# First expert layer of a two-layer mixture of experts: token rows picked by TensorE in blocks of 32 instead of scattered to memory and read back in blocks of 64

## The chip, the cores and the metric

The kernel runs on one core of a Trainium2 chip. The metric is the device time of one execution in microseconds. TensorE does the matrix products and transposes, VectorE (DVE), ScalarE (ACT) and GpSimd (POOL) the elementwise work, and SyncE (SP) issues most of the DMAs. All numbers are fp32.

## The reference

A first model of two layers (feed forward, mixer, feed forward, gated embedding) is followed by a second one whose two layers each have attention and a mixture of 32 experts. The change is in the experts of the second model's layer 0, where 512 tokens (256 of the sequence, 256 of the context) are routed:

```python
lg = t @ wr_g + br_g;  g = argmax(lg)                  # one of 4 groups
le_g = (t @ wr_e + br_e) of that group                 # 8 experts of it
top_v, top_i = top_k(le_g, 2)                          # two experts a token
weights = softmax(lg)[g] * softmax(top_v)
hidden = silu(x @ w_gate[e]) * (x @ w_up[e])           # x: rows of expert e, 1024 wide; hidden 512 wide
out[token] += weight * (hidden @ w_down[e])
```

Here `t` is `rmsnorm(x) * g * (1 + scale) + shift`, with shift and scale of its own for the sequence and for the context. The reference's own routing of its inputs gives the 32 experts of layer 0 these numbers of rows: 39 32 34 30 33 35 34 43, 35 39 27 38 41 37 29 38, 32 31 29 27 37 22 22 34, 32 33 31 30 26 24 29 21, 1,024 in all. In layer 1 (256 tokens) no expert has more than 26.

## The kernel before

Each engine has a program of its own, and semaphores order them. The three weights of an expert (gate, up, down, 2 MB each) are loaded by SP into nine slots, three experts deep: `sp_experts` issues the loads of expert e+3 when `moe_ended` of expert e is up. In layer 1 ten slots are used (`sp_experts_rows`).

Layer 0 before the change. The output projection `pe_project_out` (L1754) makes eight column tiles, VectorE adds them to x (L1767), and the sums of squares follow each (L1370). Then `act_modulated` and `dve_modulated` make the normed tokens (L1404, L1409, L1391), `pe_router` makes the logits (L1960) and turns all tokens to rows (L1971, copied out at L1994), and `dve_router` chooses experts and places (`dve_choice`, L2009 to L2078). GpSimd scatters every token's row twice into the buffer `expert_in` in memory (`pool_scatter`, L2104). Both buffers in memory are zeroed long before, in the first model's mixers (L875).

The expert loop runs one block of 64 rows a turn; the number of blocks of an expert is known only on the chip, so each expert has a loop whose two bounds are loaded to registers of each engine (`first_block`, L2110). With the counts above every expert has one block. Each turn: gate and up products (L2155; two groups of 64 columns at a time), the next block's rows turned (L2121, copied out at L2129), silu on ScalarE (L2185), the product with up on VectorE (L2203), its transpose (L2162, copied out at L2208), the down products (L2169), and the result copied by ScalarE (L2189) and written by its DMA queue to `expert_out` in two DMAs (L2192). ScalarE also loads the rows of the block after the next (L2136). L2172 ends an expert. After the last one GpSimd gathers two rows a token (L2218, L2221), and they are weighed, turned and added (L2229, L2238, L2244).

Layer 1 already works with blocks of 32 rows. Its loop has gate and up (L2468, four groups of 32 columns at a time), a pick of the next block's rows (L2429) copied out by ScalarE (L2515) and turned (L2436), a transpose (L2486) copied out at L2580, the down products (L2492), and two `pe_put` steps (L2444) with their own transposes (L2480), which layer 0 does not get. Silu is L2513, the product with up L2576.

Of the kernel before, what the change touches and what calls it, by code (L numbers as in the profile page):

```python
# [24 lines left out]
BLOCK = (64, 32)  # L25
LAM_INIT = 0.8 - 0.6

MAXROWS = max(bl * NE + 2 * n for bl, n in zip(BLOCK, (2 * S, S)))
# [5 lines left out]
class Signal:  # L34
# [29 lines left out]
    "pe_router": "r_logits r_turned r_rows_turned r_counted r_summed", "pe_moe": "moe_ended moe_turned", "pe_rows": "xr_turned xr_prepared acc_done",  # L64
# [4 lines left out]
    "act_moe": "moe_weighed", "act_rows": "xr_squared xr_out xr_root", "act_final": "final_squared final_root",  # L69
# [5 lines left out]
    "dve_moe": "moe_combined moe_added", "dve_rows": "xr_step", "dve_final": "final_step",  # L75

    "pool_setup": "zeros_set upad_zero", "pool_squares": "squares conv_u", "pool_moe": "pool_ended",
# [5 lines left out]
slot0 slot1 slot2 slot3 slot4 slot5 slot6 slot7 slot8 slot9 const3 gain_in sink_in router_in gathered0 gathered1 gathered2 gathered3 scattered stored  # L83
""".split()

BLOCKS = "x_in x_turned x_ready gated silu hidden h_turned h_ready down y_ready y_out".split()
# [29 lines left out]
def second_constants():  # L116
# [15 lines left out]
    def window(q0):  # L132
# [5 lines left out]
        "multiples": np.tile(np.arange(1, 8), (P, 1)), "swa0": window(0), "swa1": window(P),  # L138
# [20 lines left out]
class Kernel:  # L159
# [35 lines left out]
    def first_memory(self):  # L195
# [43 lines left out]
        self.xbuf = self.nc.dram_tensor("expert_in", [MAXROWS + 2 * P, D], F32).ap()  # L239
# [20 lines left out]
    def second_memory(self):  # L260
# [22 lines left out]
        self.router_cols = (KT + 1) * 36  # L283
# [554 lines left out]
def sp_mixer(k, l):  # L838
# [32 lines left out]
    for buf in (k.xbuf, k.ybuf):  # L871
        n = buf.shape[0] // P // DEPTH
        rows = buf.rearrange("(n p) d -> p n d", p=P)
        for d in (0, D // 2):
            sp.dma_start(rows[:, l * n:(l + 1) * n, d:d + D // 2], k.zeros.unsqueeze(1).broadcast_to([P, n, D // 2])).then_inc(*s["zeroed"].up(l, d, buf is k.xbuf))  # L875
# [868 lines left out]
def pe_project_out(k, l, first, slots, src, ntok):  # L1744
    pe, s = k.nc.tensor, k.s
    for j in range(KT):
        slot = slots[j // 4]
        w = chunk_view(k, slot, 512)
        if j % 4 == 0:
            pe.wait_ge(*s[f"slot{slot}"].at("chunk", first + j // 4))  # L1750
        if j >= 4:
            pe.wait_ge(*s["out_added"].at(l, j - 4))
        for t in range(KT):
            last = pe.matmul(k.ps[:, j % 4, 0:ntok], w[:, t, (j % 4) * P:(j % 4 + 1) * P], src[:, t, 0:ntok], start=(t == 0), stop=(t == KT - 1), skip_group_check=True)  # L1754
        last.then_inc(*s["out_tile"].up(l, j))
        if j > 0:
            pe_sums(k, f"moe{l}", j - 1, ntok)
    pe_sums(k, f"moe{l}", KT - 1, ntok)


def dve_project_out(k, l, streams):
    V, s = k.nc.vector, k.s
    for j in range(KT):
        V.wait_ge(*s["out_tile"].at(l, j))
        for st in streams:
            X = k.x[:, j, st * S:(st + 1) * S]
            last = V.scalar_tensor_tensor(X, k.ps[:, j % 4, st * S:(st + 1) * S], k.mod_col(l, 2, j, st), X, ALU.mult, ALU.add)  # L1767
        last.then_inc(*s["out_added"].up(l, j))


def act_project_out(k, l, ntok):
    act, s = k.nc.scalar, k.s
    for j in range(KT):
        act.wait_ge(*s["out_added"].at(l, j))
        act_square(k, f"moe{l}", j, ntok)


# [3 lines left out]
class Routing:  # L1781


    def __init__(self, k, l):
        self.numbers(l)
        self.V, self.at, self.end = k.Vflat, k.router_cols, 4096 - 2304
        self.wr, self.bias = self.V[:, 0:KT * 36].rearrange("p (k e) -> p k e", k=KT), self.V[:, KT * 36:k.router_cols]
        self.count_banks = (0, 5, 6)
        self.choice_tiles()
        nt = self.nt  # L1790
        self.idest, self.started = self.small(2, nt).bitcast(I32), self.small(len(BLOCKS))
        kf = self.V[:, 4096 - 2304:]
        BL, F, W = self.BL, self.F, self.W
        self.logits = kf[:, 0:self.T]
        self.xe = kf[:, 0:W]
        self.xeT = kf[:, 512:512 + KT * BL].rearrange("p (k s) -> p k s", k=KT)
        self.sil = kf[:, 1024:1024 + F]
        self.hb = kf[:, 1280:1280 + F]
        self.hT = kf[:, 1536:1536 + 4 * BL].rearrange("p (f s) -> p f s", f=4)
        self.yb = kf[:, 1792:1792 + W]  # L1800
        self.rows = k.Qflat[:, 0:nt * D].rearrange("p (t d) -> p t d", t=nt)
        self.g2 = k.Kflat.rearrange("p (t d) -> p t d", t=4)
        self.n = {n: Signal(k, f"moe{l}_{n}", [k.stack.enter_context(k.nc.semaphore(f"moe{l}_{n}")), 0]) for n in BLOCKS}

# [6 lines left out]
    def choice_tiles(self):  # L1811
# [7 lines left out]
        self.over = self.small(8)  # L1819
        self.pos, self.dest = self.small(nt, 32), self.small(2, nt)  # L1820
        self.ge = self.small(nt, 4)

    def small(self, *shape):
        n = int(np.prod(shape))
        v = self.V[:, self.at:self.at + n]
# [64 lines left out]
def expert_slots(e):  # L1890
    return ((2, 3, 4), (5, 0, 1), (6, 7, 8))[e % 3]
# [962 lines left out]
```

## Time and profile before

| | us |
|---|---|
| three runs, median (range) | 3088.99 (3086.84 to 3089.89) |
| the profiled execution's own time | 3092.75 |
| its span, first to last instruction | 3091.4 |
| first gate product of layer 0's experts starts | 1819.85 |
| last down product of layer 0's experts ends | 2352.9 |
| granted clock, mean of the span | 0.952 |

Times in the rows below are microseconds from the start of the span. The difference of 1.35 between the own time and the span lies outside the instructions. A shift of everything behind layer 0's experts moves the time by as much.

### The profile page before, as it was taken

To read this page: it belongs to the slowest core of one execution; us is meant where nothing else is said; L and a number is where in the kernel's file an instruction comes from. 1 tells how busy PE (TensorE), PEld (TensorE's weight loads), DVE (VectorE), ACT (ScalarE), POOL (GpSimd) and SP (SyncE) were. 2 spreads that over 40 slices of the span, in tenths; PEclk is the share of its full clock that TensorE was granted. 3 is DMA by queue.
4 is the path that set the end of the run, shared out by engine and by line. 5 is a ranking of instruction groups with operands and counts; after the bars stand their busy time and mean duration, and the time that the engine had idled before them with its cause. 6 is when DMAs were issued, how large, how long until landed. Compare 5 with 4: busy or idle time off the path is not lost.

```text
span 3091.4 us, 43046 instructions
## 1 busy us (share of the span) xinstructions
PE 2688.8 (87%) x17970; PEld 1901.5 (62%) x17970; DVE 723.0 (23%) x1844; ACT 462.0 (15%) x1096; POOL 103.8 (3%) x146
## 2 busy tenths in 40 slices
PE   8999999999999999997997868777775998877676
PEld 7888788887888688883445434343433566544454
DVE  2003420022003420023128221000002253332223
ACT  2001310011002310012016120000001142000001
POOL 1001010011001010010000010000001000000000
PEclk9999999999999999998999979989997998999989
DMA  7544765556544765525120169999997214999997
GB/s 266 189 144 146 265 219 181 168 172 204 179 135 164 262 218 195 186 86 202 55 82 1 55 234 398 397 402 398 398 397 262 92 55 171 371 420 419 420 419 310
DMA packets 257036, 721.47 MB, mean 233 GB/s; under 512 B 14207, under 2 KB 141902, under 8 KB 232270
## 3 DMA queue, kind: packets, MB, share of 16 engines
q1 hardware_dynamic: 237760, 691.74, 59.7%
q10 hardware_dynamic: 16782, 18.60, 1.9%
q0 software_dynamic: 2304, 8.39, 0.7%
q8 instruction: 145, 2.38, 0.3%
q14 instruction: 45, 0.37, 0.0%
HBM read 678.84 MB, written 39.85 MB: 232 GB/s over the span
## 4 chain that ended last, share of the span: by engine, by line
PE 71%; DMA 16%; DVE 6%; ACT 3%; issue 3%; ACTq 0%; POOL 0%; SPq 0%; DVEq 0%; POOLq 0%
PE ps L663 18%; DMA arena<-in_moe_w_up 15%; PE ps L674 10%; PE ps L1444 6%; PE ps L2155 5%; PE ps L2468 3%; PE ps L1490 2%; PE ps L2169 2%; PE ps L895 2%; PE ps L687 2%; PE ps L1055 2%; PE ps L1754 2%; PE ps L2429 1%; PE ps L2492 1%; PE ps L2274 1%
## 5 line engine op out<-in xcount | busy, mean ns | idle before, releaser
L663 PE MATMUL ps<-arena 128*128 128x256 f32 x2560 | 568.6, 379 | 3.5 <-DVE arena L745 3.5
L663 PEld LDWEIGHTS ps<-arena 128*128 128x128 f32 x2560 | 482.9, 189 | 73.9 <-issue 4.1
L2155 PE MATMUL ps<-arena 128*64 128x256 f32 x2048 | 259.3, 416 | 78.9 <-issue 77.9
L674 PE MATMUL ps<-arena 128*128 128x256 f32 x1408 | 317.9, 379 | 0.0
L674 PEld LDWEIGHTS ps<-arena 128*128 128x128 f32 x1408 | 264.8, 189 | 46.2 <-issue 8.4
L2155 PEld LDWEIGHTS ps<-arena 128*64 128x64 f32 x2048 | 159.8, 150 | 166.5 <-issue 107.3
L2468 PE MATMUL ps<-arena 128*32 128x128 f32 x4096 | 143.3, 299 | 75.8 <-issue 74.2
L1444 PE MATMUL ps<-arena 128*128 128x512 f32 (+2 forms) x512 | 192.8, 548 | 11.3 <-ACT arena L1391 11.2
L787 DVE TENSOR_TENSOR arena<-arena,ps 128x256 f32<-128x256 f32 x76 | 32.0, 422 | 638.4 <-ACT arena L755 633.8
L2468 PEld LDWEIGHTS ps<-arena 128*32 128x32 f32 x4096 | 128.6, 121 | 85.2 <-issue 83.3
L1444 PEld LDWEIGHTS ps<-arena 128*128 128x128 f32 (+1 forms) x512 | 89.4, 179 | 104.9 <-issue 97.5
L2169 PE MATMUL ps<-arena 128*64 128x512 f32 x512 | 117.0, 596 | 18.1 <-issue 18.1
L2203 DVE TENSOR_TENSOR arena<-arena,ps 128x256 f32<-128x256 f32 x32 | 19.2, 599 | 479.6 <-ACT arena L2185 479.6
L755 ACT ACTIVATE arena<-ps 128x256 f32<-128x256 f32 x76 | 29.2, 384 | 675.1 <-PE ps L663 675.1
L2492 PE MATMUL ps<-arena 128*32 128x256 f32 x1024 | 62.1, 381 | 35.9 <-DVE arena L2580 35.9
L2169 PEld LDWEIGHTS ps<-arena 128*64 128x64 f32 x512 | 40.2, 136 | 74.2 <-issue 74.2
L532 POOL TENSOR_TENSOR arena<-arena 128x256 f32<-128x256 f32 x64 | 42.8, 671 | 1079.9 <-DVE arena L500 1070.6
L895 PE MATMUL ps<-arena 128*128 128x256 f32 x352 | 77.4, 379 | 0.0
L2429 PE MATMUL ps<-arena 128*32 128x256 f32 x528 | 70.4, 637 | 7.6 <-issue 4.3
L895 PEld LDWEIGHTS ps<-arena 128*128 128x128 f32 x352 | 66.3, 189 | 9.5
L2492 PEld LDWEIGHTS ps<-arena 128*32 128x32 f32 x1024 | 36.1, 109 | 53.9 <-issue 42.3
L1490 PE MATMUL ps<-arena 128*128 128x512 f32 (+1 forms) x192 | 69.2, 520 | 0.0
(411 smaller groups left out, 2811.6 us busy)
## 6 DMA issues: line engine op xcount, KB each, us to landing
arena<-in_moe_w_gate SPq DMA_DIRECT2D x64, 2048.0 KB, 31.3
arena<-in_moe_w_up SPq DMA_DIRECT2D x64, 2048.0 KB, 31.1
arena<-in_moe_w_down SPq DMA_DIRECT2D x64, 2048.0 KB, 34.9
arena<-in_mod_w SPq DMA_DIRECT2D x24, 2048.0 KB, 13.4
arena<-in_w_gate SPq DMA_DIRECT2D x44, 1024.0 KB, 5.5
arena<-in_w_up SPq DMA_DIRECT2D x44, 1024.0 KB, 8.1
arena<-in_w_down SPq DMA_DIRECT2D x44, 1024.0 KB, 4.9
expert_in<-arena SPq DMA_DIRECT2D x4, 3328.0 KB, 14.6
```

What stands on the lines that cost most here:

```text
L663: last = pe.matmul(k.ps[:, T % 4, off:off + S], w[:, t, T % 2 * P:(T % 2 + 1) * P], h[:, t, :], start=(t == 0), stop=(t == KT - 1), skip_g ...
L674: last = pe.matmul(acc[:, t, :], d[:, T % 2, t * P:(t + 1) * P], k.hid[:, T % 4, :], start=(T == 0 and t % 2 == 0), stop=end, skip_group_c ...
L687: last = pe.matmul(k.ps[:, T, off:off + S], w[:, t, T * P:(T + 1) * P], k.hu[:, t, :], start=(t == 0 and off == 0), stop=(t == KT - 1), sk ...
L895: last = pe.matmul(dst, w[:, t, j * P:(j + 1) * P], src[:, t, :], start=(t == 0), stop=(t == KT - 1), skip_group_check=True)
L1055: last = pe.matmul(k.banks(4, 4, S)[:, j, :], w[:, t, (j % 2) * P:(j % 2 + 1) * P], k.y[:, t, :], start=(t == 0), stop=(t == KT - 1), skip ...
L1444: last = pe.matmul(k.ps[o:o + m, j % 4, 0:ntok], w[:, t, c0:c0 + m], k.h2[:, t, 0:ntok], start=(t == 0), stop=(t == KT - 1), tile_position ...
L1490: last = pe.matmul(k.ps[:, 6 + n % 2, 0:m], k.h2[:, i, t * P:(t + 1) * P], w[:, i, :], start=(i == 0), stop=(i == KT - 1), skip_group_chec ...
L2155: last = pe.matmul(ps[BL * q:BL * q + BL, b, 0:F], m.xeT[:, t, :], wv[:, t, F * q:F * q + F], start=(t == 0), stop=(t == KT - 1), tile_pos ...
L2169: last = pe.matmul(ps[BL * q:BL * q + BL, 3, 0:W], m.hT[:, f, :], wd[:, f, W * q:W * q + W], start=(f == 0), stop=(f == 3), tile_position= ...
L2429: last = k.nc.tensor.matmul(k.ps[32 * q:32 * q + 32, bank, 0:256], m.pick[:, t, :], rows, start=(t == 0), stop=(t == 1), tile_position=(0, ...
L2468: last = pe.matmul(ps[BL * q:BL * q + BL, 0, a:a + F], m.xeT[:, t, :], wv[:, t, F * q:F * q + F], start=(t == 0), stop=(t == KT - 1), tile ...
L2492: last = pe.matmul(ps[BL * q:BL * q + BL, 3, 0:W], m.hT[:, f, :], wd[:, f, W * q:W * q + W], start=(f == 0), stop=(f == 3), tile_position= ...
```

## The change

The tokens are no longer normed and modulated as columns. While the output projection runs, TensorE also makes the logits from x itself with weights multiplied by the gains, sums of squares by one-column products, and transposes of x times its gain; the shift is made into rows once. ScalarE copies the turned halves out (the second with the factor 1/rms), GpSimd adds the shift, and the token rows stay on chip (`rows`, in the space of h). The scatter, the buffer `expert_in`, its zeroing and its loads go away.

Blocks have 32 rows. VectorE makes a 0/1 matrix of places (`dve_places`), TensorE multiplies it with the rows (`pe_pick_rows`), ScalarE copies the block, TensorE turns it (`pe_turn_picked`), VectorE copies it out. The pick and the turning of the next block stand behind the down products of this one. The result is written in four DMAs of 32 KB instead of two of 128 KB. Expert 2's down weights take slot 9 instead of 8, and its three loads wait for the rows' making, the last column's turning and the projection's end. The loads of layer 1's projection weights wait for experts 30 and 31 instead of for the gathers. The zeroed part of `expert_out` becomes smaller.

```diff
-BLOCK = (64, 32)
+BLOCK = (32, 32)
-        self.xbuf = self.nc.dram_tensor("expert_in", [MAXROWS + 2 * P, D], F32).ap()
 def expert_slots(e):
-    return ((2, 3, 4), (5, 0, 1), (6, 7, 8))[e % 3]
+    return ((2, 3, 4), (5, 0, 1), (6, 7, 9))[e % 3]
...
+def pe_token_sums(k, m, i):
+    pe.wait_ge(*s["out_added"].at(0, i))
+    for t in range(4):
+        pe.matmul(k.ps[:, 3, 36 * t:36 * t + 36], k.x[:, i, t * P:(t + 1) * P], m.wp[:, t // 2, i, :], start=False, stop=(i == KT - 1), skip_group_check=True)
+    pe.wait_ge(*s["xs_squared"].at(i))
+    for t in range(4):
+        last = pe.matmul(k.ps[:, 3, 144 + t:145 + t], k.sqb[:, i % 4, t * P:(t + 1) * P], k.c["ones"][:, 0:1], start=False, stop=(i == KT - 1), skip_group_check=True)
...
+def pool_rows(k, m):
+    for t in range(4):
+        pool.wait_ge(*s["xs_out"].at(t, 1))
+        row = permuted(m.rows[:, t, :], 1)
+        pool.tensor_tensor(row, row, permuted(m.shift_rows[:, t // 2, :], 1), ALU.add).then_inc(*s["rows_made"].up(t, 1))
+    for t in range(4):
+        pool.wait_ge(*s["xs_row"].at(t))
+        row = permuted(m.rows[:, t, :], 0)
+        pool.tensor_tensor(row, row, permuted(m.shift_rows[:, t // 2, :], 0), ALU.add).then_inc(*s["rows_made"].up(t, 0))
...
+def pe_pick_rows(k, m):
+    for t in range(4):
+        for q in range(4):
+            last = k.nc.tensor.matmul(k.ps[32 * q:32 * q + 32, 1, 0:256], m.pick[:, t, :], m.rows[:, t, 256 * q:256 * q + 256], start=(t == 0), stop=(t == 3),
+                                      tile_position=(0, 32 * q), skip_group_check=True)
...
+        with pe.Fori(first_block(k, m, e, ENG.PE), first_block(k, m, e + 1, ENG.PE)) as g:
+            pe.wait_ge(*m.step("x_ready", g, 1, 1))
...
+            pe.wait_ge(*m.step("hidden", g, 1, 1))
+            pe.transpose(ps[:, 2, 0:P], m.hb, k.c["ident"])
+            pe.wait_ge(*m.step("h_ready", g, 1, 1))
...
+            pe.wait_ge(*m.step("picks", g, 5, 3))
+            pe_pick_rows(k, m)
+            pe.wait_ge(*m.step("x_out", g, 2, 1))
+            pe_turn_picked(k, m)
...
+            act.activation(m.sil, ps[:, 0, 0:m.F], ACT.Silu)
+            act.wait_ge(*m.step("down", g, 1, 1))
+            act.wait_ge(*m.step("y_out", g, 0, 64))
             act.activation(m.yb, ps[:, 3, 0:W], ACT.Copy).then_inc(m.n["y_ready"].sem, 1)
+            act.wait_ge(*m.step("x_picked", g, 2, 1))
+            act.activation(m.xe, ps[:, 1, 0:256], ACT.Copy).then_inc(m.n["x_out"].sem, 1)
+            for q in range(4):
                 act.dma_start(k.ybuf[bass.ds(g * BL, BL), W * q:W * q + W], m.yb[BL * q:BL * q + BL, :])
...
-    sp_chunk(k, 8, 2, columns(w, 0))
+    sp_chunk(k, 8, 2, columns(w, 0), s["moe_ended"].at(0, "expert", 30))
-    sp_chunk(k, 11, 5, columns(w, D + S, S))
+    sp_chunk(k, 11, 5, columns(w, D + S, S), s["moe_ended"].at(0, "expert", 31))
```

## Rows read from the trace of the kernel before

**Rows 1.** Stretches: us, busy by engine, PE clock, DMA share, GB/s.
```profile
1836.00:1970.00 134.00, 111.97 (x792) 61.20 (x792) 13.95 (x27) 8.83 (x18) 0.00 (x0) 0.95 1.00 393
...
2770.00:2900.00 130.00, 91.46 (x1679) 60.56 (x1671) 36.69 (x140) 9.39 (x27) 0.00 (x0) 0.95 1.01 419
```

**Rows 2.** Chain that ended last, layer 0's experts: start, us, what.
```profile
2177.58 37.66 DMA arena<-in_moe_w_up
2216.58 8.63 PE ps L2155 x64
...
2246.18 37.50 DMA arena<-in_moe_w_up
```

**Rows 3.** Timeline from the projection to the first expert.
```profile
1710.45 14.03 PE L1754 MATMUL ps<-arena 128*128 128x512 f32 x32 [1.21 <-ACT arena L1714]
...
1789.26 0.31 DVE L2026 TENSOR_TENSOR arena<-ps,arena 128x144 f32<-128x144 f32 x1 [0.53 <-PE ps L1964]
...
1790.97 2.04 ACT L1994 ACTIVATE arena<-ps 128x512 f32<-128x512 f32 x4
...
1799.70 0.29 DVE L2078 TENSOR_REDUCE arena<-arena 128x4 f32<-128x128 f32 x1
```

**Rows 4.** Costs of steps like those added: lines, with mean ns.
```profile
L2320 PE MATMUL ps<-arena 128*128 128x36 f32 x32 | 4.1, 268 | 0.0
...
L1224 POOL TENSOR_TENSOR arena<-arena 128x512 f32<-128x512 f32 x2 | 2.9, 1461 | 197.0 <-DVE arena L1198 197.0
```

**Rows 5.** TensorE, layer 0, one block and the start of the next.
```profile
1836.18 7.13 PE L2155 MATMUL ps<-arena 128*64 128x256 f32 x64
...
1844.59 0.44 PE L2162 MATMUL ps<-arena 128*128 128x128 f32 x2 [0.70 <-DVE arena L2203]
1845.59 3.65 PE L2169 MATMUL ps<-arena 128*64 128x512 f32 x16 [0.56 <-issue]
...
1849.33 7.14 PE L2155 MATMUL ps<-arena 128*64 128x256 f32 x64
```

**Rows 6.** Layer 1, one block of 32 rows, several engines.
```profile
2630.35 0.38 ACT L2515 ACTIVATE arena<-ps 128x256 f32<-128x256 f32 x1 [2.25 <-PE ps L2429]
...
2634.92 3.71 PE L2468 MATMUL ps<-arena 128*32 128x128 f32 x128 [0.25 <-issue]
...
2638.76 0.28 ACT L2513 ACTIVATE arena<-ps 128x128 f32<-128x128 f32 x1 [7.05 <-PE ps L2468]
2639.16 0.29 DVE L2576 TENSOR_TENSOR arena<-arena,ps 128x128 f32<-128x128 f32 x1 [1.28 <-ACT arena L2513]
```

**Rows 7.** Layer 1, TensorE alone, behind that block.
```profile
2643.68 1.94 PE L2492 MATMUL ps<-arena 128*32 128x256 f32 x32 [1.12 <-DVE arena L2580]
2645.77 3.71 PE L2468 MATMUL ps<-arena 128*32 128x128 f32 x128 [0.15 <-issue]
...
2662.53 2.91 PE L2468 MATMUL ps<-arena 128*32 128x128 f32 x62 [2.17 <-issue]
...
2725.20 1.74 PE L2468 MATMUL ps<-arena 128*32 128x128 f32 x55
...
2745.14 1.45 PE L2468 MATMUL ps<-arena 128*32 128x128 f32 x24 [3.51 <-issue]
```

**Rows 8.** DMA queues from 2640 to 3040: packets, MB, share.
```profile
q8 instruction: 44, 0.72, 0.7%
```

**Rows 9.** VectorE's loop line L2199: duration ns, first and last start.
```profile
L2199 DVEq COMPARE_BRANCH  x32: 43/43/61, 1832.0 to 2348.8; - x32
```

**Rows 10.** Results written (L2192), all of layer 0; then those after 2353.
```profile
DMA to landing us min/median/max: 2.3/9.0/11.3
...
expert_out<-arena ACTq DMA_DIRECT2D x2, 128.0 KB, 2.3
```

**Rows 11.** TensorE's waits before 1500: total us, times, longest.
```profile
PE ps L377 <- DMA arena<-in_x: 7.3, 1, 7.3
```

**Rows 12.** SP's issue of the next layer's projection weights.
```profile
2373.15 9.63 SPq L1355 DMA_DIRECT2D arena<-in_b_w_qkv  x4
```

More of the change, by code:

```diff
@@ L1761, in dve_project_out @@
[L1761 to L1775, printed above, removed]
@@ L1781 @@
-class Routing:
[L1784 to L1803, printed above, removed]
+class Routing:
@@ new lines, in pe_picked_factors @@
+def pe_picked_factors(k, m):
+    pe, s, ps = k.nc.tensor, k.s, k.ps
+    pe.wait_ge(*s["xs_step"].at("factors"))
+    pe.matmul(ps[:, 3, 0:72], k.c["ones"], m.wsum, start=True, stop=True, skip_group_check=True).then_inc(*s["xs_prepared"].up("bias"))
+    for st in range(2):
+        for half in range(2):
+            pe.matmul(ps[:, 4 + 2 * st + half, :], k.c["ones"], m.shifts[:, st, 4 * half:4 * half + 4, :], start=True, stop=True,
+                      skip_group_check=True).then_inc(*s["xs_prepared"].up(st, half))
@@ new lines, in pe_turn_scaled, with permuted @@
+def pe_turn_scaled(k, m, i):
+    pe, s = k.nc.tensor, k.s
+    pe.wait_ge(*s["xs_scaled"].at(i))
+    if i == 0:
+        pe.wait_ge(*s["xs_shift"].at(1, 1))
+    if i == 4:
+        pe.wait_ge(*s["xs_out"].at(3, 0))
+    for t in range(4):
+        last = pe.transpose(k.ps[:, 4 + t, (i % 4) * P:(i % 4 + 1) * P], m.scaled[:, i % 2, t * P:(t + 1) * P], k.c["ident"])
+    last.then_inc(*s["xs_turned"].up(i))
+def permuted(row, half):
+    return row.rearrange("p (b j a) -> p b j a", b=KT, j=KT)[:, :, 4 * half:4 * half + 4, :]
@@ new lines, in dve_project_picked @@
+def dve_project_picked(k, m):
+    V, s = k.nc.vector, k.s
+    for j in range(KT):
+        V.wait_ge(*s["out_tile"].at(0, j))
+        for st in range(2):
+            X = k.x[:, j, st * S:(st + 1) * S]
+            last = V.scalar_tensor_tensor(X, k.ps[:, j % 3, st * S:(st + 1) * S], k.mod_col(0, 2, j, st), X, ALU.mult, ALU.add)
+        last.then_inc(*s["out_added"].up(0, j))
+        if j == 0:
+            dve_picked_factors(k, m)
+        if j == 1:
+            V.wait_ge(*s["xs_prepared"].at("bias"))
+            for st in range(2):
+                last = V.tensor_tensor(m.bias2[:, st, :], k.ps[:, 3, 36 * st:36 * st + 36], m.bias, ALU.add)
+            last.then_inc(*s["xs_step"].up("bias"))
@@ new lines, in act_router_picked @@
+def act_router_picked(k, m):
+    act, s, l = k.nc.scalar, k.s, m.l
+    act.wait_ge(*s["r_dve"].at(l, "group"))
+    act.activation(m.ge, m.ge, ACT.Exp).then_inc(*s["r_act"].up(l, "group"))
+    act.wait_ge(*s["xs_out"].at(3, 0))
+    for t in range(4):
+        row = permuted(m.rows[:, t, :], 0)
+        act.activation(row, row, ACT.Copy, scale=m.r[:, t:t + 1]).then_inc(*s["xs_row"].up(t))
+    act.wait_ge(*s["r_dve"].at(l, "second"))
+    act.activation(m.m2, m.m2, ACT.Exp).then_inc(*s["r_act"].up(l, "second"))
+    act.activation(k.lnA[:, 1, KT:KT + 1], k.eps, ACT.Silu)
@@ new lines, in dve_router_picked @@
+def dve_router_picked(k, m):
+    V, s, ps = k.nc.vector, k.s, k.ps
+    r = s["r_dve"]
+    for i, name in enumerate(PICKED_BLOCKS):
+        V.memset(m.started[:, i:i + 1], 0.0).then_inc(*m.n[name].up())
+    V.wait_ge(*s["xs_root"].at())
+    V.reciprocal(m.r, m.r).then_inc(*s["xs_step"].up("factor"))
+    V.wait_ge(*s["xs_step"].last())
+    for t in range(4):
+        V.scalar_tensor_tensor(m.lg[:, t, :], ps[:, 3, 36 * t:36 * t + 36], m.r[:, t:t + 1], m.bias2[:, t // 2, :], ALU.mult, ALU.add).then_inc(*r.up())
+    dve_choice(k, m)
```

409 lines of the change are left out of this document (212 added, 197 removed).

## Prediction

> **What bounds the kernel now.** Only the experts of layer 0 and their two ends are touched, so I read the stretches first, then the chain through that stage, then the timeline of its opening, then one block. The stretches show DMAs fully busy at 393 GB/s [rows 1]. The chain shows the same: a load takes 37.6 us, and the issue of one load to that of the load four experts later takes 2246.18 - 2177.58 = 68.6 us, 17.15 an expert [rows 2]. One block of 64 takes TensorE 13.15 us (1836.18 to 1849.33) [rows 5]. So weights set the pace, with 4 us an expert to spare on TensorE. Before the stage, DMAs stand still: the first gate product starts at 1819.85 although the places are known at 1799.99 [rows 3]; scatter and reading back fill the 20 us.
>
> **Part 1, the opening.** The projection starts at 1710.45; two of its eight tiles take 14.03 us with the pipeline's end, so 6.88 a tile or 0.86 for each of its eight products [rows 3]: 8 x 6.88 = 55.0. Per column tile come four logit products and four one-column ones, whose 32 records of 0.27 overlap in pairs [rows 4], about 0.24 a product in a stream, so 1.9, and four transposes at 0.12 to 0.22 [rows 5], so 0.5: 2.4 x 8 = 19. The shift's products add 4 x 0.86 and their preparation about 1. With 1 us of waiting for the last column all sums are there at 1710.5 + 55.0 + 19 + 4.4 + 1 = 1790. The choice then begins at about 1791.5, against 1789.26, lasts 10.7 us as before (1789.26 to 1799.99) [rows 3], and the places' matrix takes 0.8: 1803. GpSimd adds the shift in eight steps of 1.46 = 11.7 us [rows 4], behind ScalarE's table load and first copy (0.51 each) [rows 3], from about 1792.4: 1804.1, the later of the two. Pick, copy, turning and copy (below) end at 1809. The first gate product is 10.8 us earlier than 1819.85. If strided rows or the shared port make GpSimd slower by half, it is 5 us.
>
> **Part 2, a block.** From gate start, by layer 1's block [rows 6, 7]: gate and up 3.71; silu starts 3.84, lasts 0.28; product with up from 4.24, 0.29; transpose at 4.6 (0.22 to 0.27); copy 0.28; down from 5.3, 1.94; the pick has the same shape and count as the down products (128x256, 32 records), so 1.9, and follows with no wait, since VectorE made its matrix a block earlier; end at 9.1. Then nothing covers what comes: ScalarE's copy 0.38 [rows 6], two transposes 0.44 [rows 5], VectorE's copy about 0.4, four hand-overs of about 0.07: next gate at 10.5. In front of a new expert the two loop bounds are read, which starts only when the turning has been issued: 11.1. Before, the turning lay under silu and product.
>
> The counts of rows make 47 blocks of 32: experts 0 to 15 have 28, experts 16 to 31 have 19. 32 blocks at 11.1 and 15 second blocks at 10.5 are 513 us, against 533 before (1819.85 to 2352.9). So halved blocks with a longer tail win nothing inside the loop; a floor price that is hardly under today's is the first fact of this case.
>
> **Part 3, instructions.** The floor isn't reached in layer 1. In one stream of six blocks the gate products start at 2645.77 and at 2725.20: 13.2 us a block, where the undisturbed one takes 10.85 (2634.92 to 2645.77) [rows 6, 7]. No engine releases TensorE in the gaps; they lie in the middle of the gate products (2.17 at 2662.53, up to 3.51 at 2745.14) [rows 7] and come once or twice in 400 instructions. In the 400 us from 2640 the instruction queue fetched 44 pieces of 16 KB [rows 8], 1.6 for each of 27 blocks, each piece about one us of one engine (0.7% of 16 x 400 / 44). I read the gaps as waits for the next piece while weights fill the DMA engines. Layer 0's block of 64 has 88 product records and none of these gaps; the new block has 197, nearly layer 1's 199. The gaps of these six blocks sum to 2.0 a block. First blocks run under full DMAs: 1.6, so 12.7. Second blocks run partly with idle DMAs: 0.9.
>
> The 15 second blocks need a jump back over about 400 instructions. No trace shows one: the loop's branch is there 32 times for 32 experts, 43 ns each, never taken back [rows 9]. From below it costs 0.04; from above two pieces at the longest gap, 2 x 3.5 = 7.0 [rows 7]. I take one piece, 2.3, like the usual gap, because 1.6 pieces a block leave the loop's head at least one piece behind. A second block is 10.5 + 0.9 + 2.3 = 13.7.
>
> The Trainium skill, Runtime: NRT & Kernel Launch, section Instruction fetch mechanics, speaks against the change: a jump taken to an instruction outside the two pages at hand must first fetch the target page by DMA. By that rule the jump costs a page, as I took; without it the jump is free and the sum is that of rival B. No row here shows a jump back.
>
> **Part 4, the sum.** Last gate start: 1809 + 1.5 (clock low after the opening) + 31 x 12.7 + 15 x 13.7 = 2409.7; its down products end 8.7 later: 2418.4, against 2352.9: +65.5. DMAs don't bind then: a load without x and y traffic costs 6.29 MB / 419 GB/s = 15.0 [rows 1], the 2.1 us above that are today's 512 KB of x and y an expert; by bytes a new block's 128 KB cost 0.5, by packets 1.1. 32 x 15.0 + 47 x 0.8 = 518, less than 609.
>
> The end is later by more. Results leave ScalarE behind its copy of the pick (+2) in four issues (+1.2). Today the last ones land in 2.3 us on idle DMAs; under load they take 9.0 [rows 10], and now 10 MB of projection weights are issued at the ends of experts 30 and 31, not at 2373.15 [rows 12], into that moment. +3 to +13, I take +8. Those weights weren't waited for, so their early start gives nothing. The zeroing taken out (13 MB) lay beside products: TensorE's only long DMA wait ahead of 1500 is for the input [rows 11]; 0. Smaller results' zeroing: 0. Expert 2's loads start at 1804 instead of 1785 to 1794 and end by 1820, before they are needed; 0.
>
> 65.5 + 8 = +73.5 on the execution's own 3092.75, which is 3.76 over the median 3088.99. On the median: 3162.5; I say **3160**.
>
> **The rivals.**
> A, the other side: TensorE's gaps don't appear. Then the floor holds: 28 blocks to expert 15 end at 2115, from there 14 loads follow one another, 14 x 15.0 + 19 x 0.5 to 1.1, and the last expert ends at 2337 to 2348. With the end at +3 to +8 the time is 3076 to 3092. For it: GpSimd, VectorE and ScalarE are nearly idle and x's traffic is gone. Against it: six blocks of layer 1 in a row. It decides when gaps and jumps together stay under 0.3 us a block. Chance 0.18, of which 0.12 faster.
> B, gaps but a free jump: second blocks 11.4, 35 us less: 3128. Chance 0.20. The change doesn't do what a halved block promises, but the loss is half.
> C, a dear jump: two pieces, 7.0 instead of 2.3: +70, 3233. Chance 0.12.
> The results' landing: a block's four DMAs must land before the next block's copy. By rows 10 they take 9.0 to 11.3, from 2.8 after the down products on, so up to 14 of 12.7 to 13.7, with 1.9 of pick as slack; it adds at most 1 us a block to any case and is in the range.
>
> **Numbers.** Forecast 0.50 (alone 3130 to 3190), A 0.18, B 0.20, C 0.12. Range 3090 to 3215: it leaves out A's faster part and the dearer half of C. A change within 0.2% (6 us) can't be told from none here: faster 0.12, same 0.08, slower 0.80.
>
> **What would show it.** First gate product near 1809; the pick 1.9 us behind down; blocks of experts with one block about 12.7 apart with gaps marked as issue in the gate products; a gap of over 2 us ahead of second blocks; DMA share near 0.85 in the loop and no wait for weights; last results landing in over 5 us. Wrong would be: second blocks 10.5 to 11 apart, or TensorE waiting for weights.

## The result and the profile after

The change made the kernel slower: 3115.14 us median (3113.0 to 3123.19, 4 runs) against 3089.44 (3086.84 to 3092.22, 4 runs) beside it, a ratio of 1.0086 with a 95% interval of 1.0071 to 1.0100. The forecast was 3160: right in direction and inside the range, but it asked for 73.5 us and 25.7 came.

The stretches of layer 0's experts after the change (us, busy by engine, PE clock, DMA share, GB/s):

```profile
1817.00:1873.00 56.00, 41.97 (x981) 31.04 (x981) 9.24 (x34) 5.22 (x15) 0.00 (x0) 1.00 0.67 268
1873.00:2120.00 247.00, 184.49 (x4248) 138.23 (x4248) 36.40 (x129) 22.10 (x64) 0.00 (x0) 0.97 0.80 317
2120.00:2250.00 130.00, 95.39 (x2082) 70.18 (x2086) 18.54 (x65) 11.10 (x32) 0.00 (x0) 0.95 1.01 414
```

The share was 1.00 from 1836 to 1970 before [rows 1]; now weights leave a fifth of the DMA time unused until 2120. One second block, TensorE alone, with the start of the one behind it:

```profile
1851.45 3.71 PE L2232 MATMUL ps<-arena 128*32 128x128 f32 x128 [1.00 <-DVE arena L2276]
1856.04 0.33 PE L2237 MATMUL ps<-arena 128*128 128x128 f32 x1 [0.88 <-DVE arena L2294]
1856.80 1.94 PE L2243 MATMUL ps<-arena 128*32 128x256 f32 x32 [0.43 <-issue]
1858.53 1.94 PE L2207 MATMUL ps<-arena 128*32 128x256 f32 x32
1860.96 0.44 PE L2526 MATMUL ps<-arena 128*128 128x128 f32 x2 [0.49 <-ACT arena L2267]
1862.00 1.19 PE L2232 MATMUL ps<-arena 128*32 128x128 f32 x36 [0.59 <-DVE arena L2276]
```

Gate and up, transpose, down, pick, turning: 10.55 us, the floor of Part 2. The block that starts at 1862.00 is an expert's second: TensorE has jumped back ahead of it, and the wait is 0.59 for VectorE's copy, the hand-over alone. Over the loop the 15 intervals that end at a second block have a median of 10.55 and a mean of 11.24, the 31 that end at a first block 11.21 and 11.95.

The choice in the opening, VectorE and GpSimd:

```profile
1794.63 5.06 POOL L2158 TENSOR_TENSOR arena<-arena 128x512 f32<-128x512 f32 x4 [425.64 <-ACT arena L2114]
...
1796.06 1.21 DVE L1930 TENSOR_TENSOR arena<-arena 128x32 f32<-128x32 f32 x1
...
1797.30 0.19 DVE L1932 TENSOR_REDUCE arena<-arena 128x4 f32<-128x32 f32 x1
...
1798.54 1.20 DVE L1952 SCALAR_TENSOR_TENSOR arena<-arena 128x32 f32<-128x32 f32 x1
1799.65 5.02 POOL L2162 TENSOR_TENSOR arena<-arena 128x512 f32<-128x512 f32 x4
1799.66 1.41 DVE L1953 TENSOR_TENSOR arena<-arena 128x128 f32<-128x128 f32 x1
...
1811.13 0.17 DVE L2283 COPY arena<-arena 128x8 f32<-128x8 f32 x1
```

While GpSimd's additions (1.26 us each) run, operations with two inputs that took 0.19 to 0.3 us in the kernel before take 0.9 to 1.4; the reduction between them, with one input, takes 0.19 as before. The choice ends at 1811.1 and the first gate product starts at 1817.77, against 1819.85 before (the choice before is in [rows 3]). GpSimd's last addition ends at 1804.7, so VectorE is the later of the two.

The end of the stage, from the chain that ended last:

```profile
2328.72 26.79 DMA arena<-in_moe_w_up
2355.51 1.32 issue
2356.84 6.00 PE ps L2232 x128
...
2364.44 1.93 PE ps L2243 x32
2366.37 1.76 PE ps L2207 x32
...
2369.77 4.96 DMA expert_out<-arena
...
2384.04 12.60 DMA arena<-expert_out,arena
...
2403.98 9.77 PE ps L1369 x16
```

The last down products end at 2366.37 (2352.9 before, +13.5). From there to the next layer's first sums (L1369) it takes 37.6 us, against 28.4 before, where they began at 2381.32. The results' landing takes 4.96 instead of 2.3 [rows 10].

The balance of the span (the profiled executions), 3115.3 against 3091.4: first gate product -2.1 (with 1.9 lost ahead of the projection), loop +15.6, end of the stage +9.2, behind it +1.2: +23.9. TensorE's products ahead of the projection are the same, but for one in 7,432, yet the projection starts anywhere from 1707.2 to 1713.2 in their profiles. So below I compare stretches inside a profile, and whole kernels by their medians.

### The profile page after: what moved, and what is told of

The parts are those of the page before. It is cut to its first block, busy times and chain, and to the rows that moved or that the text cites. A ratio compares the mean times of both kernels' runs of the same rounds, so it can differ in the third digit from the quotient of the medians.

```text
span 3115.3 us, 56996 instructions
## 1 busy us (share of the span) xinstructions
PE 2694.1 (86%) x24517; PEld 2002.9 (64%) x24517; DVE 757.8 (24%) x2035; ACT 484.3 (16%) x1182; POOL 105.7 (3%) x146
## 4 chain that ended last, share of the span: by engine, by line
PE 75%; DMA 10%; DVE 6%; issue 4%; ACT 4%; ACTq 1%; POOL 0%; SPq 0%; DVEq 0%
PE ps L663 18%; PE ps L674 10%; DMA arena<-in_moe_w_up 8%; PE ps L1443 6%; PE ps L2232 5%; PE ps L2243 3%; PE ps L2207 3%; PE ps L2558 2%; PE ps L1489 2%; PE ps L894 2%; PE ps L687 2%; PE ps L2024 2%; PE ps L1054 2%; DMA expert_out<-arena 1%; PE ps L2519 1%
## 5 line engine op out<-in xcount | busy, mean ns | idle before, releaser
L2232 PE MATMUL ps<-arena 128*32 128x128 f32 x6016 | 184.5, 281 | 50.4 <-DVE arena L2276 40.7
L2558 PE MATMUL ps<-arena 128*32 128x128 f32 x4096 | 146.3, 305 | 81.1 <-issue 79.4
L2232 PEld LDWEIGHTS ps<-arena 128*32 128x32 f32 x6016 | 170.7, 113 | 57.7 <-issue 57.1
L2558 PEld LDWEIGHTS ps<-arena 128*32 128x32 f32 x4096 | 132.8, 123 | 89.4 <-issue 87.6
L787 DVE TENSOR_TENSOR arena<-arena,ps 128x256 f32<-128x256 f32 x76 | 32.1, 422 | 638.4 <-ACT arena L755 633.7
L755 ACT ACTIVATE arena<-ps 128x256 f32<-128x256 f32 x76 | 29.1, 384 | 675.2 <-PE ps L663 675.2
L2243 PE MATMUL ps<-arena 128*32 128x256 f32 x1504 | 98.4, 397 | 21.9 <-issue 21.4
L2207 PE MATMUL ps<-arena 128*32 128x256 f32 x1536 | 98.7, 390 | 3.0 <-DVE arena L2283 3.0
L2582 PE MATMUL ps<-arena 128*32 128x256 f32 x1024 | 62.3, 381 | 35.8 <-DVE arena L2670 35.8
L2243 PEld LDWEIGHTS ps<-arena 128*32 128x32 f32 x1504 | 54.2, 112 | 50.8 <-issue 34.9
L2207 PEld LDWEIGHTS ps<-arena 128*32 128x32 f32 x1536 | 62.0, 113 | 30.1 <-issue 4.6
L2276 DVE COPY arena<-ps 128x256 f32<-128x256 f32 x48 | 20.4, 425 | 243.8 <-PE ps L2526 243.8
L2519 PE MATMUL ps<-arena 128*32 128x256 f32 x528 | 69.3, 637 | 5.2 <-DVE arena L1989 3.3
## 6 DMA issues: line engine op xcount, KB each, us to landing
arena<-in_moe_w_down SPq DMA_DIRECT2D x64, 2048.0 KB, 23.2
```

What stands on the lines that cost most here:

```text
L2207: last = k.nc.tensor.matmul(k.ps[32 * q:32 * q + 32, 1, 0:256], m.pick[:, t, :], m.rows[:, t, 256 * q:256 * q + 256], start=(t == 0), stop ...
L2232: last = pe.matmul(ps[BL * q:BL * q + BL, 0, a:a + F], m.xeT[:, t, :], wv[:, t, F * q:F * q + F], start=(t == 0), stop=(t == KT - 1), tile ...
L2243: last = pe.matmul(ps[BL * q:BL * q + BL, 3, 0:W], m.hT[:, f, :], wd[:, f, W * q:W * q + W], start=(f == 0), stop=(f == 3), tile_position= ...
L2519: last = k.nc.tensor.matmul(k.ps[32 * q:32 * q + 32, bank, 0:256], m.pick[:, t, :], rows, start=(t == 0), stop=(t == 1), tile_position=(0, ...
L2558: last = pe.matmul(ps[BL * q:BL * q + BL, 0, a:a + F], m.xeT[:, t, :], wv[:, t, F * q:F * q + F], start=(t == 0), stop=(t == KT - 1), tile ...
```

## The experiments

All edits are to the changed kernel if nothing else is said, and each ratio is to the kernel before, measured beside it.

**Pick behind gate and up**

```diff
 gate and up products; gated
+pe.wait_ge(*m.step("picks", g, 5, 3)); pe_pick_rows(k, m)
 transpose of hb (L2237)
+pe.wait_ge(*m.step("x_out", g, 2, 1)); pe_turn_picked(k, m)
 down products
-pe.wait_ge(*m.step("picks", g, 5, 3)); pe_pick_rows(k, m)
-pe.wait_ge(*m.step("x_out", g, 2, 1)); pe_turn_picked(k, m)
 ScalarE: xe copy now ahead of the yb copy
```

> The changed kernel with another order inside layer 0's block: the next block's pick stands directly behind the gate and up products, its turning behind the transpose of the hidden rows, the down products last; ScalarE copies the picked rows before it copies the results. Nothing is left out. Theory S (a block is as long as TensorE's own chain, and pick and turning behind the down products are its uncovered end): second blocks come 8.6 to 8.8 us apart instead of 10.55, experts with one block 9.0 to 9.3 instead of 11.1. Theory W (weights take over): 29 experts' loads remain behind the first three and follow one another at 15.0 to 16.5 us, so the last down products end at 2270 to 2315 instead of 2366 and the time is 3020 to 3065 against 3115. Theory I (TensorE waits for instructions, as in layer 1, which has this order): gaps of 1.6 to 2.0 us a block appear because the block leaves no other slack, 47 blocks give 75 to 94 back, and the time is 3100 or more.

Measured: 3089.15 us, ratio 1.0003 (0.9993 to 1.0014). Against 3115.14 that is 26 us less, far from the 50 to 95 of theories S and W. Undisturbed blocks are 8.1 to 8.8 apart, a little less than S has it, but they are few. The chain that ended last says what took over:

```profile
1985.12 10.13 DMA expert_out<-arena
1995.28 0.40 ACT arena L2267
...
2005.57 11.51 DMA expert_out<-arena
2017.09 0.39 ACT arena L2267
...
2019.09 10.12 DMA expert_out<-arena
2029.23 0.39 ACT arena L2267
```

Copy of the results 0.39 us, four issues about 1.6, landing 10 to 11.5: 12.1 us from the second of these copies to the third, since the next copy (L2267 here) needs the buffer. These are long ones: over the loop the last landing of a block comes 4.2 to 11.9 us behind its last issue, with a median of 9.6 (the first block's, ahead of the full loads, took 1.5). 34 of the 47 copies waited for a landing. The landing that the prediction put at "at most 1 us a block" was harmless only because the block was 11 us long. None of the three theories had named it. From expert 28 on W's bound is there as well: blocks stand 14.2 to 15.4 us apart, and first gate products wait 4.2 to 5.5.

**The copy of x first**

```diff
+wait x_picked; activation(m.xe, ...)      # to x_out
 wait down, y_out; activation(m.yb, ...)   # to y_ready
-wait x_picked; activation(m.xe, ...)
```

> The changed kernel with one edit: ScalarE copies the picked rows of the next block before it copies the results, so that its wait for the landing of the last block's results no longer stands ahead of the turning. Theory L (that landing delays blocks): in the changed kernel five blocks lose 1.3 to 2.3 us each, 9 in sum, and every block's copy of the picked rows comes no later than now; the loop shortens by 5 to 9 us and the time is 3106 to 3110. Rival W (behind 2120 the DMAs are fully busy, four of the five delays stand there, and what TensorE gains it waits for weights): at most 2 us less, 3113 to 3115.

3110.27 us, ratio 1.0069 (1.0055 to 1.0083). Its loop took 544.3 us from the first gate product to the last down product, against 548.6. The waits of 1.3 to 2.3 us ahead of the turning are gone; this is how one of them looks in the changed kernel:

```profile
1896.29 0.38 ACT L2265 ACTIVATE arena<-ps 128x256 f32<-128x256 f32 x1 [6.26 <-DMA expert_out<-arena]
1896.57 0.38 ACT L2267 ACTIVATE arena<-ps 128x256 f32<-128x256 f32 x1
...
1897.00 0.47 PE L2526 MATMUL ps<-arena 128*128 128x128 f32 x2 [2.09 <-ACT arena L2267]
```

A copy waits 6.26 us for a landing, the next copy stands behind it, and TensorE waits 2.09 for that one. The sign fits theory L, but the next kernel's loop, untouched, is 3.4 us shorter as well, and the interval overlaps that of the changed kernel: 5 us is as much as this can be, and it is not established. TensorE's waits say where most of it went. Ahead of the turning they fall from 29.1 to 22.6 us in the loop, but ahead of the transpose (L2237) they rise from 40.5 to 45.3, the longest from 0.9 to 3.0: now the next block's silu stands behind the copy that waits for the landing.

**Projection weights wait for the gathers**

```diff
+sp.wait_ge(pool_ended); sp.wait_ge(gathered0 to gathered3)
-sp_chunk(k, 8, 2, columns(w, 0), s["moe_ended"].at(0, "expert", 30))
+sp_chunk(k, 8, 2, columns(w, 0))
-sp_chunk(k, 11, 5, columns(w, D + S, S), s["moe_ended"].at(0, "expert", 31))
+sp_chunk(k, 11, 5, columns(w, D + S, S))
```

> The changed kernel with one edit: layer 1's six projection pieces (10 MB) wait for the eight gathers of the combination, as in the kernel before, and are not issued at the ends of experts 30 and 31. Theory C (they collide with the last results' landing and with the gathers): from the last down products to TensorE's first transpose of the combination it takes 28 to 31 us again instead of 37.6, and unless the next layer's projection then waits for its weights, the time is 3106 to 3109. Rival P (the longer tail is the four issues of 32 rows and the copy of the pick ahead of them): 34 us or more remain. In either case the projection of layer 1 may wait up to 5 us for weights that are now late.

3102.51 us, ratio 1.0040 (1.0024 to 1.0057). Its TensorE at the end:

```profile
2361.05 1.93 PE L2243 MATMUL ps<-arena 128*32 128x256 f32 x32 [0.43 <-issue]
2362.78 1.94 PE L2207 MATMUL ps<-arena 128*32 128x256 f32 x32
...
2377.63 1.97 PE L2346 MATMUL ps<-arena 128*128 128x128 f32 x8 [11.83 <-DVE arena L2328]
...
2392.10 1.22 PE L1369 MATMUL ps<-arena 128*128 128x512 f32 x1 [2.83 <-ACT arena L1376]
```

From the last down products (2362.98) to the next layer's first sums (2392.10) it is 29.1 us, and before it was 28.4. (The 37.6 of the text above is measured to these sums as well, not to the first transpose that it names.) The results' four DMAs now land in 1.5 us each. Theory C holds: nearly the whole longer tail is 10 MB of weights issued into the results' landing and the gathers. Rival P is out, and nothing waited for the weights that now come later. The time is below the 3106 that was expected; 3.4 us of it lie in the loop, which this edit doesn't touch.

**Few additions on GpSimd**

```diff
-pool.tensor_tensor(row, row, shift, ALU.add)
+pool.tensor_tensor(row[..., 0:1], row[..., 0:1], shift[..., 0:1], ALU.add)
```

> The changed kernel with GpSimd's eight additions of the shift cut to one sixteenth of their elements, so the rows that layer 0's experts see lack most of the shift, and layer 1 may choose other experts; only the opening is to be read. Theory G (GpSimd's additions slow the choice on VectorE): the choice takes 10.7 to 11.5 us again instead of 17.7, its operations with two inputs 0.19 to 0.3 us instead of 0.9 to 1.4, and the first gate product starts at 1810 to 1812 instead of 1817.8. Rival D (the choice is longer for a reason of its own, such as ScalarE's table loads and its copies): it stays at 16 us or more.

In the trace the choice takes 11.1 us, from 1792.02 to 1803.12, instead of 17.7, and the first gate product starts at 1809.58. Theory G holds. VectorE's rows for two of the operations above:

```profile
1794.33 0.19 DVE L1930 TENSOR_TENSOR arena<-arena 128x32 f32<-128x32 f32 x1
...
1795.00 0.25 DVE L1952 SCALAR_TENSOR_TENSOR arena<-arena 128x32 f32<-128x32 f32 x1
```

**Three buffers for the results**

```diff
-one yb, one semaphore y_out
+yb[e % 2] with a semaphore each for an expert's first block
+yb[2] with a third semaphore for its further blocks
 (ScalarE's block once outside the loop, once in it; the rest as in the pick behind gate and up)
```

> The kernel of e1_pick_behind_gate with one more edit: ScalarE copies an expert's first block of results into one of two buffers in turn and every further block's into a third, each with a semaphore of its own, so that a copy no longer waits for the landing of the block before. Its loop body stands twice in ScalarE's program. Nothing is left out. Theory L (in e1 the cycle copy 0.39, issue 2.0, landing 10 makes 12.4 us a block): blocks come 8.6 to 9.3 us apart until TensorE waits for weights; then 29 loads of an expert follow one another from 1822 on at 15.0 us and 0.3 to 1.1 a block of results, the last down products end at 2280 to 2320 instead of 2338, and the time is 3030 to 3072 against 3089 for e1. Rival I (instructions): faster blocks need their instructions sooner than the loaded queue brings them; gaps of 2 us a block replace the landing's waits and the time stays at 3085 or more.

3055.26 us, ratio 0.9892 (0.9877 to 0.9907): faster than both kernels. No copy waits for a landing any more. The landing was the bound of most of the reordered loop. Its stretches:

```profile
1873.00:2120.00 247.00, 218.87 (x5114) 162.75 (x5105) 44.87 (x157) 30.73 (x95) 0.00 (x0) 0.97 1.01 409
2120.00:2250.00 130.00, 101.62 (x2214) 75.33 (x2205) 20.32 (x71) 14.15 (x44) 0.00 (x0) 0.92 1.02 419
```

TensorE is at 89% of the first stretch and the DMAs are full; the last experts stand 14.5 to 16 us apart, their first products wait 4 to 5 us, and the chain that ended last holds the last load of `in_moe_w_up` for 32.06 us. The last down products end at 2308.6, inside theory L's 2280 to 2320. Rival I is not wholly out: twelve gaps of 1.4 to 3.9 us (29 in all) stand inside the blocks, and they are part of why only about half of the blocks are 8.7 us or less.

**The kernel before with blocks of 32**

```diff
-BLOCK = (64, 32)
+BLOCK = (32, 32)      # before.py; the counting of blocks up to 15 instead of 7
```

> The kernel before with one edit: layer 0's blocks have 32 rows instead of 64 (47 blocks instead of 32 or so); scattering and reading back through device memory stay. It tells what the block size alone does. Theory N (a round trip bounds each block: the x rows are loaded only after the last turning, the results must land before the next copy, and each landing takes 9 to 10 us under load): blocks come at 12 to 12.4 us, 47 of them take 565 to 585 us instead of 533, and the time is 3120 to 3145. Rival W (weights set the pace at 17.15 us an expert whatever the block): 3085 to 3095.

3112.04 us, ratio 1.0083 (1.0069 to 1.0096), the same loss as the whole change. TensorE's waits from 1820 to 2350 (total us, times, longest):

```profile
PE ps L2121 <- DMA arena<-expert_in: 128.1, 29, 6.2
PE ps L2169 <- issue: 21.8, 45, 0.7
```

The down products behind such a wait, and behind the next one without a wait:

```profile
1903.02 0.69 PE L2121 MATMUL ps<-arena 128*128 128x128 f32 x2 [4.53 <-DMA arena<-expert_in]
...
1904.47 3.64 PE L2169 MATMUL ps<-arena 128*32 128x256 f32 x32 [0.55 <-issue]
...
1913.99 1.94 PE L2169 MATMUL ps<-arena 128*32 128x256 f32 x32 [0.43 <-issue]
```

Theory N names the right mechanism, round trips through memory, and the loop of 556.5 us (1815.93 to 2372.39) is a little shorter than its 565 to 585, and so the time is under its 3120. The waits cost more than their own length: the granted clock of the loop is 0.79, against 0.92 in the kernel before and 0.96 in the changed one. Behind the wait of 4.53 us it is 0.50 from 1903 to 1908, the lower of its two levels (1.2 instead of 2.4 GHz), and the down products take 3.64 us; the next ones, with no such wait ahead of them, take 1.94. Halving the blocks costs what the change costs; picking on chip removes these 128 us of waiting, and the low clock with them, and puts pick and turning on TensorE's uncovered path instead.

**Buffers and waiting weights together**

```diff
 the three buffers, and the edit of the projection weights
```

> e5_three_result_buffers together with the edit of e3_projection_waits (layer 1's projection pieces wait for the gathers). Nothing is left out. If the two edits add up, it is 8 to 12 us faster than e5: 3020 to 3062, and faster than the kernel before by 0.9 to 2.2%. Rival: with a loop that ends on waits for weights, the DMAs are free at the end only if the projection waits, so the gain is the whole 12; or the projection's TensorE now waits for its own weights and half of it is lost.

3046.11 us, ratio 0.9866 (0.9851 to 0.9881). The tail is 28.4 us (2306.82 to 2335.20) instead of 36.6; the edits add up.

**A quarter of the experts' weights**

```diff
+half = src.shape[-1] // 4
+dst, src = dst[..., 0:half], src[..., 0:half]
 sp.dma_start(dst, src)
```

> The changed kernel with the experts' weight loads of both layers cut to a quarter of their bytes (the rest of each matrix keeps what the buffer held before, so the output and layer 1's routing are not the reference's; times are read from the trace). DMA share in layer 0's loop falls under 0.4. Theory F (a piece of instructions is fetched in time unless the DMA engines are full; gaps come only where its fetch takes longer than the piece before lasts): TensorE's gaps of 1 us and more vanish in both layers, landings of results take 2 to 3 us, first blocks stand 11.1 and second blocks 10.55 us apart throughout, gate products of layer 0 span 500 to 504 us, and layer 1's blocks stand 10.85 apart instead of 13.2. Rival P (the gaps belong to the program and come per piece whatever the load): layer 1 keeps about 1 gap of 2 us a block.

Layer 0's loop, from the first gate product (1818.38) to the last down product (2367.91), takes 549.5 us: what it takes with full weights. Both theories lose something here. TensorE's waits in layer 1, the changed kernel from 2660 to 3060 and then this one from 2660 to 2980:

```profile
PE ps L2558 <- issue: 71.4, 30, 4.4
PE ps L2582 <- DVE arena L2670: 31.4, 28, 1.2
```

```profile
PE ps L2584 <- DVE arena L2672: 32.5, 29, 1.2
PE ps L2560 <- issue: 2.2, 7, 0.6
```

In layer 1 the gaps are gone and blocks stand 11.0 apart instead of 14.5, so those did come from the full DMAs. The timeline parts them in two kinds: 19 of the 30, with 50 of the 71 us, stand ahead of a block's first gate product, where the program waits for its weights and blocks come 15 us apart; 11, with 21 us, stand inside the gate products, where it waits for no semaphore. In layer 0 the gaps stay, at the same product of the same experts. Expert 12's first block in the changed kernel, and with a quarter of the weights:

```profile
2056.74 2.35 PE L2232 MATMUL ps<-arena 128*32 128x128 f32 x74
2061.73 0.65 PE L2232 MATMUL ps<-arena 128*32 128x128 f32 x6 [2.65 <-issue]
```

```profile
2056.98 3.67 PE L2234 MATMUL ps<-arena 128*32 128x128 f32 x122 [1.02 <-DVE arena L2278]
2063.32 0.42 PE L2234 MATMUL ps<-arena 128*32 128x128 f32 x6 [2.67 <-issue]
```

Six records are left behind the gap in both. Expert 19 has 23 left (2.96 and 4.06 us), expert 29 ten (1.44 and 3.38). A place doesn't give a gap in every execution: of the five profiles with this order and place of the program, all show those of experts 12, 17 and 29, three that of expert 19, three another in expert 4, one in expert 2.

Full DMAs alone don't bring layer 1's kind. From 2126 to 2356 layer 0 of the changed kernel has a share of 0.99 to 1.01 too, and the only gaps of over 1.2 us marked as issue inside its blocks are those of experts 17, 19 and 29, which stay with a quarter of the weights.

**Short additions on GpSimd**

```diff
-pool.tensor_tensor(row, row, shift, ALU.add)
+for b in range(0, 8, 2):
+    pool.tensor_tensor(row[:, b:b + 2], row[:, b:b + 2], shift[:, b:b + 2], ALU.add)
 (on the kernel of buffers and waiting weights)
```

> e7_buffers_and_waits with one edit: each of GpSimd's eight additions of the shift is issued as four of 128 columns. Nothing is left out. Theory G (a VectorE operation with two inputs waits until GpSimd's running addition is over): the waits shrink with the additions, VectorE's 128x32 operations take 0.3 to 0.5 us instead of 0.9 to 1.4, the choice 12 to 13.5 us instead of 17.7, the first gate product starts 4 to 5 us earlier, near 1813, unless GpSimd, itself held up more often, becomes the later one; the whole kernel gains 2 to 5 us, 3041 to 3044. Rival D (the two engines share a port in fixed proportion, whatever the length of an instruction): the choice stays at 17 us and the time at 3046.

The choice takes 13.3 us (1785.14 to 1798.45), and the first gate product starts at 1805.78; 6 of the 12.8 us by which that is earlier than in the kernel before this one lie ahead of the projection. The same operations again:

```profile
1787.45 0.33 DVE L1932 TENSOR_TENSOR arena<-arena 128x32 f32<-128x32 f32 x1
...
1788.26 0.36 DVE L1954 SCALAR_TENSOR_TENSOR arena<-arena 128x32 f32<-128x32 f32 x1
1788.54 0.59 DVE L1955 TENSOR_TENSOR arena<-arena 128x128 f32<-128x128 f32 x1
```

An addition about a third as long (0.45 us instead of 1.26) takes the wait of the 128x128 operation from 1.13 us to 0.31, so theory G holds: VectorE waits out one addition at a time. GpSimd's additions now take 14 us in all instead of 10 and run on beside VectorE's later steps, and there copies with one input are longer too: 0.32 us instead of 0.18 (128x32), 0.40 instead of 0.17 (128x8). So it isn't operations with two inputs alone; the reductions stay as they were. The kernel is at 3039.62 us, ratio 0.9850 (0.9834 to 0.9867), the fastest here; its gain over the one before it is within the intervals.

**The program moved**

```diff
 pe_project_picked(...)
+for i in range(24):
+    pe.matmul(ps[0:32, 2, 511:512], ident[:, 0:32], ident[:, 0:1])
 pe_count(...)
```

> The changed kernel with 24 idle one-column products on TensorE behind the projection, while VectorE makes the choice; nothing waits for them. They move all of TensorE's later instructions by 96 places. Nothing is left out. In the changed kernel and in e8 TensorE stands still for 2 to 4 us in the first blocks of experts 12, 17, 19 and 29, at the same product each time, and for 1 us in expert 10. Theory A (these gaps belong to places of the program in memory): they move to other products, about a quarter of a block earlier in the order of instructions, or to other experts. Rival B (they belong to what those experts do, such as a block count before them): they stay in the same experts at the same product. The time changes by less than 4 us, 3111 to 3119, either way.

One run, 3113.01 us; loop 551.9 us. Theory A: the gaps of over 2 us moved to experts 8, 13, 15, 25 and 30, and experts 12, 17, 19 and 29 have none. Since experts 12, 17 and 29 show theirs in all five profiles of the unmoved program, chance is a poor reading of that. Two of the new ones:

```profile
2080.92 0.38 PE L2232 MATMUL ps<-arena 128*32 128x128 f32 x2 [2.67 <-issue]
2118.47 0.92 PE L2232 MATMUL ps<-arena 128*32 128x128 f32 x25 [3.33 <-issue]
```

**Buffers with a quarter of the weights**

```diff
 the three buffers, and the cut of the weight loads
```

> e5_three_result_buffers with the experts' weight loads of both layers cut to a quarter of their bytes, as in e8 (output and layer 1's routing are not the reference's; layer 0's loop is read from the trace). It takes the weights off the bound of the best loop. Theory W (e5's loop ends on waits for weights): the intervals of 15.2 to 15.4 us behind 2260 fall to 8.3 to 9, and layer 0's 47 blocks take 400 to 420 us from the first gate product to the last down product instead of 490. Rival I (such short blocks can't be supplied with instructions, whatever the load): gaps of 2 us and more in most blocks, and 450 us or more.

One run; layer 0's loop takes 419.9 us (1817.63 to 2237.48), against 490.2 in the kernel with three buffers and full weights. Theory W: most intervals are 8.1 to 8.5. So the full loads of weights cost that loop 70 us, and instructions can be had at 8.3 us a block. Eight gaps of 1.4 to 2.4 us (16 in all) are left, against twelve (29) with full weights.

## Why the direction was right and the size wrong

**What bounds the kernel before** stood. So did **Part 2**: 11.1 and 10.5 were forecast as the floor, and 11.12 and 10.55 are the undisturbed intervals.

**Part 3 failed**, in both terms. For the gaps I took six blocks of layer 1 [rows 7] and carried them, at 1.6 us, to every first block: 12.7. The 31 measured average 11.95, so 31 x 0.75 = 23 us too much. (The six blocks' gaps sum to 9.55, which is the 1.6 a block; the 2.0 of the text holds a seventh block's.) Those six blocks stand in a stretch with a DMA share of 1.02 (2645 to 2726), and with a quarter of the weights layer 1 has no gap of over 0.6 us. Layer 0's DMAs are at 0.67 to 0.80 until 2120, and behind that, at 1.01, its blocks still don't show them. Its own gaps are of another kind: five or so in the loop, tied to where the program lies (they stay when weights go, and move when the program moves).

For the jump back I took one piece, 2.3, and with 0.9 of gaps a second block of 13.7; the 15 measured average 11.24, so 15 x 2.46 = 37 us too much: the 2.3 of the jump wasn't there, and the gaps were 0.7. The jump costs nothing that a row shows: 0.59 us of waiting ahead of a second block, with the wait put down to VectorE. The instruction queue fetched 173 pieces in the whole kernel and 145 before, 28 more. An estimate of what the longer program alone asks for: before, TensorE ran 35,940 records (products and weight loads), 248 for each of the 145 pieces; the new bodies hold 32 x 109 more product records, each with its weight load, 6,976 in all or 28 pieces. That leaves none for fifteen jumps.

My own sign of being wrong, second blocks 10.5 to 11 apart, is what the trace shows. These two terms are 60 us too much; the opening, 9 too little, took part of that back, and the forecast ended 48 us too high. That the time still lies inside the range is owed to the range's width and to that, not to the mechanism. Rival B, with its free jump, was nearer (3128), and I had given it 0.20.

The Trainium skill, Runtime: NRT & Kernel Launch, section Instruction fetch mechanics, has the rule that I followed (a jump outside two pages must fetch), and also says that TensorE's instruction memory holds 2,048 instructions. By the second figure a jump over 400 would find its target there, and the trace agrees with that one: at fifteen jumps it shows no wait and no piece fetched.

**Part 1 was off by 9 us** the other way. The sums were there at 1792.1, which is the 1790 of the forecast and the 1.9 us lost ahead of the projection, and then the choice took 17.7 us, not 10.7 "as before". I had asked whether the shared port makes GpSimd slower and had its additions as the later of the two paths (1804.1; they ended at 1804.7), and it is VectorE that waits: 11.1 us when the additions are a sixteenth, 13.3 with short ones. The Trainium skill, SBUF — State Buffer, section SBUF: two separate sides, says that the pair of ports shared by the two engines is an exclusive lock held for a whole instruction, and that VectorE needs it in its modes that use both ports and, beside a GpSimd operation that reads SBUF, for operations with two SBUF inputs. Both experiments and the 0.19 of the reductions agree. The low clock was there too, but ahead of the first gate product: with TensorE nearly idle during the choice, 0.50 was granted from 1800 to 1815, the lower level, and the opening's pick took 3.47 us instead of 1.94.

**Part 4.** The end was +8 and measured +9.2, and the weights issued early were the reason: 8.5 of it go away when they wait. That the DMAs don't bind in the loop was right, more than I had meant: a quarter of the weights leaves the loop at 549.5 us.

By terms, the last gate product was forecast for 2409.7 and came at 2356.84: opening +8.8, slow clock -1.5 (it lies in the opening), first blocks -23.2, second blocks -36.9. **Rival A**, faster without gaps, failed too: it had the last expert end at 2337 to 2348, with weights as the bound from 2115 on. TensorE's own chain stayed the bound until the last expert, which waited about 2 us for its weights. Of the 36 us that the intervals are over their floors, five blocks with gaps of over 1 us at fixed places hold about 19, the results' landing about 6, and the wait for the last weights about 2; the rest is small gaps and slow stretches. The direction held because the floor of 11.12 and 10.55 is only about 20 us under the old loop: 36 us of gaps and 9 us at the end are enough to turn that round.

**What stays open:** why only some experts show a gap. In the changed kernel and in the moved one nearly all fall between the 103rd and the 145th product record of a first block, which is what a piece of some 250 instructions that begins near the loop's head would give at its end. That is a reading of positions, and no run tested it. Also open is why layer 1's blocks have gaps inside their gate products under full DMAs when layer 0's, with 197 product records against 199, don't, and what picking on chip would have given with blocks of 64, which no run tried.

## What to carry to other kernels

A block's floor on TensorE is a sum of what lies behind it and isn't covered. Here the same steps in another order, with buffers enough that no store is waited for, take 8.3 us instead of 11.1 and turn +0.86% into -1.1%. When a loop gets shorter, list every round trip in it with its loaded latency (a median of 9.6 us here, 1.5 without load): the one that was hidden is the next bound. And a price taken from another stage belongs to that stage only: look at the DMA share of both before carrying it over, and even where the shares are alike, look for one block that shows it.

## What the runs showed of the hardware

Of four DMAs of 32 KB the last lands 4.2 to 11.9 us behind its issue beside full weight loads (median 9.6, the reordered loop) and in 1.5 on idle engines; two of 128 KB took 2.3 there [rows 10]. A jump back over some 400 of TensorE's instructions costs nothing visible. An operation of VectorE with two inputs from SBUF waits for the end of GpSimd's running addition (0.19 us becomes 1.2 with additions of 1.26, 0.33 with additions of 0.45), and some copies with one input do too (0.17 became 0.40), while reductions don't. TensorE stopped for 1.4 to 4 us at a few places of its long program, with a DMA share of 0.31 as with 0.80, and the places moved with the program. Behind a wait of 4.53 us for a load the granted clock was 0.50 for some 5 us, and TensorE's products took almost twice as long (3.64 us instead of 1.94); over a loop with 29 such waits it was 0.79.
